# An expert loop whose transposes go from TensorE to VectorE, with the weight rows regrouped to match

## The reference

```python
xin = xf[buf_tok].reshape(nblk, MOE_BLOCK, D)          # xf = RMSNorm(x) * norm2_g
def expert_block(args):
    xb, e = args
    hh = xb @ w1[e] + b1[e]                            # 1024 -> 2048
    x_glu = jnp.minimum(hh[..., ::2], SWIGLU_LIMIT)
    x_lin = jnp.clip(hh[..., 1::2], -SWIGLU_LIMIT, SWIGLU_LIMIT)
    act = x_glu * jax.nn.sigmoid(SWIGLU_ALPHA * x_glu) * (x_lin + 1.0)
    return act @ w2[e] + b2[e]                         # 1024 -> 1024
```

## Time and profile before

| what | value |
|---|---|
| median of 3 runs | 1527.27 us (1527.02 to 1527.79) |
| profiled execution, first to last instruction | 1525.0 us |
| expert loop, first matmul to the last of block 32 | 431.65 to 1499.92 us |
| one block while nothing disturbs it | 33.14 us |
| TensorE busy | 1451.5 us, 95% of the span |
| moved by DMA | 452.72 MB, 297 GB/s over the span |
| DMA rate in the loop | 384 to 400 GB/s in most of 40 slices |

### The profile page before, as it was taken

The page is one execution under the profiler, slowest core; times in us unless marked ns, Lnnn a source line. Parts: engine busy times, 40 slices in busy tenths (PEclk is TensorE's granted clock), DMA queues, the critical chain, the costliest instruction groups (busy, mean ns, idle before and its releaser), DMA issues.

```text
span 1525.0 us, 33907 instructions
## 1 busy us (share of the span) xinstructions
PE 1451.5 (95%) x14155; PEld 644.4 (42%) x14155; DVE 412.5 (27%) x988; ACT 280.7 (18%) x545; POOL 244.5 (16%) x342
## 2 busy tenths in 40 slices
PE   6999989799589999999999999999999999999995
PEld 3344447444534433334443334444333444443332
DVE  1008152622432222223222223222222322222233
ACT  3413022431101111111111111111111111111112
POOL 0000000000002221112122111223111222221111
PEclk9999995799689999999999999999999999999997
DMA  9110000260559999999999999999999999999983
GB/s 359 45 49 0 0 25 25 83 261 0 221 190 364 384 388 394 399 394 398 391 388 388 397 399 400 396 386 392 390 396 394 400 398 378 393 387 392 388 324 118
DMA packets 103864, 452.72 MB, mean 297 GB/s; under 512 B 16543, under 2 KB 25175, under 8 KB 71076
## 3 DMA queue, kind: packets, MB, share of 16 engines
q1 hardware_dynamic: 82232, 426.54, 70.5%
q0 software_dynamic: 17728, 16.86, 5.5%
q10 hardware_dynamic: 3884, 9.04, 1.6%
HBM read 442.63 MB, written 18.91 MB: 303 GB/s over the span
## 4 chain that ended last, share of the span: by engine, by line
PE 84%; DMA 8%; DVE 5%; ACT 1%; issue 1%; POOL 0%; SPq 0%; DVEq 0%; POOLq 0%
PE bank L691 40%; PE bank L699 19%; DMA arena<-in_w 7%; PE bank L483 6%; PE bank L476 5%; PE bank L623 4%; PE bank L730 2%; PE bank L684 1%; PE bank L569 1%; PE bank L576 1%; PE bank L604 1%; DVE fixed L1085 1%; PE bank L632 1%; ACT fixed L902 1%; DVE arena L1120 1%
## 5 line engine op out<-in xcount | busy, mean ns | idle before, releaser
L691 PE MATMUL bank<-arena,fixed 128*32 128x512 f32 x6144 | 669.6, 594 | 3.8 <-DMA arena<-in_w 2.8
L691 PEld LDWEIGHTS bank<-arena,fixed 128*32 128x32 f32 x6144 | 202.9, 110 | 451.0 <-issue 445.7
L699 PE MATMUL bank<-arena,fixed 128*32 128x256 f32 x6144 | 351.4, 381 | 0.0
L1303 DVE TENSOR_TENSOR fixed<-bank,fixed 128x512 f32<-128x512 f32 x96 | 66.4, 692 | 788.0 <-PE bank L691 788.0
L699 PEld LDWEIGHTS bank<-arena,fixed 128*32 128x32 f32 x6144 | 189.7, 110 | 129.9 <-issue 10.7
L823 POOL DMA_INDIRECT sum_d<-fixed x96 | 150.5, 1568 | 15.1 <-issue 14.2
L976 ACT ACTIVATE fixed<-fixed 128x256 f32<-128x256 f32 x96 | 43.2, 450 | 560.6 <-DVE fixed L1304 560.6
L799 POOL COPY fixed<-fixed 96x1 int32 (+1 forms) x34 | 6.1, 179 | 635.2 <-PE bank L684 614.5
L786 POOL TENSOR_TENSOR fixed<-fixed 128x1 f32<-128x1 f32 x130 | 63.3, 487 | 205.5 <-ACT fixed L997 202.6
L483 PE MATMUL bank<-arena,fixed 128*128 128x512 f32 x192 | 85.7, 609 | 0.0
L476 PE MATMUL bank<-fixed,arena 128*128 128x512 f32 x192 | 82.8, 592 | 0.8 <-DVE fixed L1045 0.8
(11 more groups left out here) (191 smaller groups left out, 807.3 us busy)
## 6 DMA issues: line engine op xcount, KB each, us to landing
arena<-in_w SPq DMA_DIRECT2D x384, 1024.0 KB, 16.9
arena<-in_w_in SPq DMA_DIRECT2D x6, 2048.0 KB, 16.1
arena<-in_w_out SPq DMA_DIRECT2D x1, 4096.0 KB, 21.6
fixed<-rel_d ACTq DMA_DIRECT2D x8, 448.0 KB, 3.7
fixed<-in_x SPq DMA_DIRECT2D x4, 512.0 KB, 6.3
hn_d<-fixed ACTq DMA_DIRECT2D x1, 2048.0 KB, 7.0
sum_d<-fixed ACTq DMA_DIRECT2D x1, 2048.0 KB, 13.2
fixed<-sum_d SPq DMA_DIRECT2D x4, 512.0 KB, 5.1
```

Source lines behind the costliest of these rows:

```text
L691: m = pe.matmul(bank[r][GR * j:GR * (j + 1), :], XT[:, k, GR * r:GR * (r + 1)], W1[:, k, 512 * j:512 * (j + 1)], start=k == 0, stop=k == N ...
L699: m = pe.matmul(bank[3 + r // 2][GR * j:GR * (j + 1), 256 * (r % 2):256 * (r % 2 + 1)], ATT[:, r, c, f2, :], W2[:, 2 * f2 + c, 256 * j:256 ...
L1303: step(v.tensor_tensor(z, bank[r][:, :], B1T, ALU.add))
```

## The change

VectorE now does both kinds of transpose, in blocks of 32 x 32. Such a transpose turns each 32 x 32 block in its place: from `ACTV`, partition 32j + i of `ATT` gets value 256j + 8i + f for f = 0 to 7 when the source columns are read with stride 8, which is value 8p + f for partition p. So the rows of a weight matrix that belong to one partition must be the eight consecutive ones 8p to 8p + 7. The weight loads follow: partition p of slot k gets row 8p + k instead of 128k + p.

- Tokens: `XG` holds quarter rows. Three indirect DMAs of 128 quarter rows (1 KB) each gather a block's tokens, by the scatter's table `SID`; the table `TOK` and its instruction go. Three VectorE transposes (128 x 256) write `XT`.
- Activations: after each group's product, VectorE transposes `ACTV[:, r, :]` into `ATT[:, r]`. TensorE's transposes and ScalarE's copies go.
- TensorE's products run in plain order r = 0, 1, 2, each over f = 0 to 3.
- Weights: `w1` slot k is read as 128 rows of 8 KB that lie 64 KB apart (before: 1 MB in one stretch). A piece of `w2` is read as 128 runs of 8 KB (two consecutive rows), 32 KB apart (before: 256 rows of 4 KB, in one stretch of 1 MB).
- `norm2_g` is now multiplied into `HN` (one `scalar_tensor_tensor` in place of a `tensor_scalar`, L1196 before), from a broadcast row `G2` (512 KB, a new DMA on ScalarE's queue between the router's weights and its bias); the scaling of the router's weights goes.

```diff
-    XG = view(fixed, o_qk, D, parts=SLOTS)
-    XT = view(fixed, o_qk + 1024, NK, SLOTS)
+    XG = view(fixed, o_qk, NG, D // NJ)
+    XT = view(fixed, o_qk + 1024, NG, NK, GR)
...
             for k in range(NK):
-                             w1[bass.ds(e, 1), k * P:(k + 1) * P, :].rearrange("e p n -> (e p) n")
+                             w1[bass.ds(e, 1), :, :].rearrange("e (p k) n -> (e p) k n", k=NK)[:, k, :]
...
             for f in range(NF // 2):
-                             w2[bass.ds(e, 1), 2 * f * P:(2 * f + 2) * P, :].rearrange("e (a p) n -> p (e a) n", p=P)
+                             w2[bass.ds(e, 1), :, :].rearrange("e (p f) n -> (e p) f n", f=NF)[:, 2 * f:2 * f + 2, :]
...
-            act_transposes(0)
-            x_transposes(16 * g + 32)
-            pe.wait_ge(s_at, NG * g + 1)
...
+            for r in range(NG):
+                pe.wait_ge(s_at, NG * g + r + 1)
+                for f2 in range(NF // 2):
+                    if r == 0:
+                        pe.wait_ge(s_w2[f2], 16 * g + 16)
+                    m = product(r, f2)
+                    if r == 2:
+                        m.then_inc(s_used, 1)
+                if r == 1:
+                    m.then_inc(s_yf, 1)
...
-            pool.indirect_dma_start(out=XG, out_offset=None, in_=hn_d.ap(),
-                                    in_offset=bass.IndirectOffsetOnAxis(GI, 0),
+            for r in range(NG):
+                pool.indirect_dma_start(out=XG[:, r, :], out_offset=None, in_=quarters,
+                                        in_offset=bass.IndirectOffsetOnAxis(GI[:, r:r + 1], 0),
...
+        act.dma_start(G2, bass.AP(norm2_g.tensor, 0, [[0, P], [1, D]])).then_inc(s_g2, 16)
...
-                v.tensor_scalar(HN[:, t, :], X[:, t, :], st4[:, t:t + 1], None, ALU.mult).then_inc(s_xn, 1)
+                v.scalar_tensor_tensor(HN[:, t, :], X[:, t, :], st4[:, t:t + 1], G2,
+                                       ALU.mult, ALU.mult).then_inc(s_xn, 1)
...
+            for r in range(NG):
+                v.transpose(XT[:, r, :, :], XG[:, r, :].rearrange("p (i k) -> p k i", k=NK)).then_inc(s_xt, 1)
             v.stream_shuffle(B1T, B1Q, [0] * GR).then_inc(s_b1p, 1)
...
+                v.transpose(ATT[:, r, :, :], ACTV[:, r, :].rearrange("p (i f) -> p f i", f=NF)).then_inc(s_at, 1)
```

More of the change, by code:

```diff
@@ L250, in encoder_block @@
     ACTV = view(fixed, o_nt + 2304, NG, FF // NJ)
-    ATT = view(fixed, o_gqk, NG, 2, NJ, GR)
+    ATT = view(fixed, o_gqk, NG, NF, GR)
     YN = view(fixed, o_gqk + 768, NG, D // NJ)
@@ L264, in encoder_block @@
     VT = view(fixed, take(NV), NV)
-    GI = view(fixed, take(1), 1, parts=SLOTS, dt=I32)
+    GI = view(fixed, o_l + NCL + 2 * NG * COLS, NG, dt=I32)
     SI = view(fixed, take(NG), NG, dt=I32)
@@ L284, in encoder_block @@
     JUNK = view(fixed, o_a, D)
+    G2 = view(fixed, o_a, D)
     ident = CF[:, CI:CI + P]
@@ L675, in _ @@
         assert done[0] == len(jobs)
[L678 to L686, removed]
         def hidden(r, k):
             for j in range(NJ):
-                m = pe.matmul(bank[r][GR * j:GR * (j + 1), :], XT[:, k, GR * r:GR * (r + 1)],
+                m = pe.matmul(bank[r][GR * j:GR * (j + 1), :], XT[:, r, k, :],
                               W1[:, k, 512 * j:512 * (j + 1)], start=k == 0, stop=k == NK - 1)
@@ L724, in _ @@
                     m.then_inc(s_hf, 1)
[L726 to L731, removed]
-            act_transposes(0)
-            x_transposes(16 * g + 32)
-            pe.wait_ge(s_at, NG * g + 1)
[L737 to L752, removed]
+            for r in range(NG):
[8 more added lines that the diff above has]
+                    m.then_inc(s_yf, 1)
         nb = pe.value_load(EMAP[0:1, MAXB:MAXB + 1], min_val=E, max_val=MAXB)
         pe.wait_ge(s_yn, NG * nb)
-        pe.wait_ge(s_xt, 2 * nb + 2)
+        pe.wait_ge(s_xt, NG * nb + NG)
         pe.wait_ge(s_b2, 16)
@@ L789, in _ @@
         pool.memset(B1Q, 0.0).then_inc(s_b1z, 1)
-        last_token, last_row = (pool.to_reg(n - 1) for n in (SEQ, SEQ * NJ))
+        last_row = pool.to_reg(SEQ * NJ - 1)
         pool.wait_ge(s_hst, 16)
@@ L797, in gather @@
         def gather(column, copied):
[L799 removed]
+            pool.tensor_copy(GI, SID[:, :, column].rearrange("p a b -> p (a b)")).then_inc(s_idx, 1)
             pool.wait_ge(s_idx, copied)
             hold(NG)
[L802 to L804 removed]
+            for r in range(NG):
+                pool.indirect_dma_start(out=XG[:, r, :], out_offset=None, in_=quarters,
+                                        in_offset=bass.IndirectOffsetOnAxis(GI[:, r:r + 1], 0),
+                                        bounds_check=last_row, oob_is_err=False).then_inc(s_gath, 16)
+        quarters = hn_d.ap().rearrange("t (j n) -> (t j) n", j=NJ)
         gather(slice(0, 1), 2)
[L807 removed]
+        pool.wait_ge(s_xt, NG)
         gather(slice(1, 2), 3)
[L809 removed]
         pool.wait_ge(s_acc0, 16)
@@ L1168, in _ @@
         v.wait_ge(s_rw, 48)
-        for k in range(NK):
-            ins = v.tensor_scalar(RWs[:, k, :], RWs[:, k, :], VT[:, V2 + k:V2 + k + 1], None, ALU.mult)
-        ins.then_inc(s_rw2, 1)
+        v.wait_ge(s_g2, 16)
         io = CF[:, CIO:CIO + E]
@@ L1262, in _, with next_tokens @@
         wait_empty(v, ("rep",))
[L1264 to L1276, removed]
+        def next_tokens(n):
+            v.wait_ge(s_b1, 16 * n)
+            v.wait_ge(s_gath, 16 * NG * n)
+            for r in range(NG):
+                v.transpose(XT[:, r, :, :], XG[:, r, :].rearrange("p (i k) -> p k i", k=NK)).then_inc(s_xt, 1)
             v.stream_shuffle(B1T, B1Q, [0] * GR).then_inc(s_b1p, 1)
         v.wait_ge(s_b1z, 1)
-        next_tokens(0, 16)
+        next_tokens(1)
         blocks = v.value_load(EMAP[0:1, MAXB:MAXB + 1], min_val=E, max_val=MAXB)
```

40 lines of the change are left out of this document (13 added, 27 removed).

## The result

The changed kernel takes 1490.5 us (1488.9 to 1491.0, 4 runs) where the kernel before takes 1527.4: a ratio of 0.9755, 95% interval 0.9742 to 0.9769. The gain is 37 us; 11.6 had been forecast (1515.7), and the range ended at 1500. The direction and the bound were right, the size was a third of what came.

What follows compares the result with a forecast made beforehand. The prediction took the DMA stream of weights to bound the loop. Start +3.8, HN +0.5, stream -10.4, block 1 -1.9 and tail -3.6 sum to -11.6 us: span 1525.0 to 1513.4, median 1515.7, range 1500 to 1534.

Steps and rivals of the forecast that it cites:

- The bound: Loop: the DMA stream of weights takes 33.9 us a block and bounds it; TensorE as the bound had chance 0.04.
- nearly all off the path: TensorE's transposes in the loop: removing them saves TensorE 57 us over 32 blocks, nearly all without effect on the time.
- The signs I had named: Loop, if right: blocks of 33.0 to 33.6 us, TensorE idle about 2 us in each from the first quarter on.
- The stream itself: Weight loads over the loop's 31 blocks: -10.4 us in sum; no gain there had chance 0.16.
- block 1's gap: Block 1, where the DMA ran dry before W2's slots came free: first piece free earlier, -1.9 us.
- The run length of w2: W2 loads in runs of 8 KB instead of 4 KB: -0.24 us per block, -7.4 in all, bounds -10 and 0.
- The address pattern: Weight loads with 64 KB or 32 KB pitch: taken as 0, 31 us either way; a slower stream had chance 0.15.
- The third part, the gathers: Quarter rows spread each token over four partition groups, loading DMA engines more evenly: -3 us, bounds -7.5 and +5.
- The start: Before the first hidden matmul: later first gather, three gathers, VectorE transposes, +3.8 us (2.6 to 5.3); HN ahead, +0.5.
- VectorE's cover: VectorE's transposes in each block, 0.37 to 0.74 us each, are done before TensorE needs them: no cost.
- GpSimd: "Nothing": Three gathers queue in front of each block's scatters; the last scatter still waits for TensorE's end: no cost.
- The tail: Last block: TensorE ends 8.0 us behind the last W2 landing instead of 11.6, -3.6 us.

## Why the prediction was wrong, step by step

**The bound** was named rightly: the stream, not TensorE, although TensorE was busy 95%. TensorE's 2.2 us less per block gave no 70 us. But I called them "nearly all off the path". They are off it only as long as the stream stays slower than 33.14 us a block. The three runs on the kernel before show that taking them away is what lets a faster stream count: with them, each of three ways to speed the stream ended at 1522. The signs I had named came near: blocks of 32.53 us (said 33.0 to 33.6), TensorE idle 1.4 us in each (said about 2), from block 11 of 32 on (said the first quarter).

**"The stream itself", the step that failed.** Its sum of -10.4 over 31 blocks, with -1.9 for block 1's gap, was -38.6. It had three parts. The run length of w2 was sized at -7.4 and measured 10.1. The address pattern was taken at 0 and measured 0 (1489.1 against 1490.5). The Trainium skill's page ("DMA: Bandwidth & Descriptors", Latency and other measured facts) gives figures for row pitches from 512 KiB up and none below; what the prediction calls full rate there is 207 GB/s against 214. That nothing is lost at 64 KB was my extrapolation, and these runs bear it out. The third part, the gathers, I treated only as load: the same bytes, perhaps spread better over the engines, -3 with bounds of -7.5 and +5. The run with the old gather puts them at 28.4, and 20.6 of it go with the number of partitions alone. The effect that I had priced did not come: the engines end as unevenly as before, with a share of 0.12 up to 1452. I never asked what the gather does to the packets of the weights beside it. The row that shows it was there to be read: windows of 2 us behind each gather, at 336 and 305 GB/s with the share at 1.0. My windows were whole blocks, and an average of 390 hides a dip of 4 us. The two measured parts come to 38.5, near the 38.6; but they were taken one at a time out of the changed kernel, and no run has the kernel before without TensorE's transposes alone.

**The start:** +3.8 and +0.5 forecast, the first hidden matmul came +3.2 later. Rows of the changed kernel, GpSimd's first and last gather and VectorE's transposes:

```profile
427.82 1.12 POOL L775 DMA_INDIRECT fixed<-hn_d,fixed  x1 [0.17 <-issue]
...
430.58 1.00 POOL L775 DMA_INDIRECT fixed<-hn_d,fixed  x1 [0.30 <-issue]
...
433.02 1.67 DVE L1230 STREAM_TRANSPOSE fixed<-fixed 128x256 f32<-128x256 f32 x3 [5.66 <-DMA fixed<-hn_d,fixed]
```

The first gather was issued 2.3 us later (425.50 to 427.82), where +1.2 for `SID` and +0.5 for HN had been forecast. A gather of 128 quarter rows takes 1.0 to 1.1 us, not 1.4; one of 96 rows of 4 KB in the changed kernel takes 1.06 and one over 128 partitions 1.09, so the time doesn't go by the rows. The data came 3.2 later (429.83 to 433.02), and transposing took 1.8 as before, where 1.3 was forecast. The delayed router's bias was hidden, as said: VectorE waited for it until 341.91 instead of 340.17, and the first transposes of HN moved from 353.96 to 354.34 only.

**VectorE's cover** held, in price and place:

```profile
L1266 DVE STREAM_TRANSPOSE fixed<-fixed 128x256 f32<-128x256 f32 x96 | 62.7, 654 | 3.3
L1230 DVE STREAM_TRANSPOSE fixed<-fixed 128x256 f32<-128x256 f32 x99 | 55.6, 613 | 5.7 <-DMA fixed<-hn_d,fixed 5.7
```

0.65 us is between my 0.37 and 0.74, nearer the upper one, and TensorE never waits for them in the loop. The 0.62 estimated from the Trainium skill ("VectorE: DVE Perf Modes", The three transpose paths) is near it; the page's figure is for bf16, and these transposes are float32.

**GpSimd: "Nothing"** was wrong for the last block. I had the gathers end 9 us behind the hidden part's end, with the scatters free to follow; they ended 9.9 behind 1450.6, and then three scatters of 2 us each stood in a row behind TensorE's end. In the loop that is covered, at the end nothing covers it: 2.9 us. Turning the order round gave back 1.8 of them.

**The tail** of the stream was right in mechanism and near in size, 8.6 us behind the last landing for the 8.0 forecast.

**The range** failed for the same reason as the sum: its lower end took the bounds of the known effects and left no room for one that I hadn't looked for.

## What to carry to other kernels

Two bounds within 2% of each other hide each other: a faster stream alone gave 5 us, TensorE's transposes gone beside the old gather 9 (w2's longer runs included), both 37. Before judging a change to one of them, work out what each alone would allow. When the DMA's share is full, look at its rate too, in windows as short as the smallest transfer in the loop and over many iterations, not in one: here a stretch at full share with a lower rate was a transfer that held up its neighbours, and a single block showed it less surely than 27. And where a gather runs beside a stream of loads, try it over all 128 partitions, with its rows laid so that empty ones are spread evenly.

## What the runs showed of the hardware that was not expected

- In the kernel before, a gather of some 64 rows of 4 KB, declared over 96 partitions, pulled the weight stream beside it from 423 to 336 and 305 GB/s for 4 us with the share at 1.0; declared over 128 partitions it left it at 412 and 408. In the changed kernel the same step made 31 blocks 20.6 us shorter, though there a dip of 2 us stayed, at 299 GB/s with a share of 0.86.
- Loads in runs of 8 KB instead of 4 KB: 0.33 us less per 4.19 MB. A pitch of 64 KB between 8 KB rows: no difference.
- In the run with the old gather TensorE waited for weights 24 times, and behind eight of these waits, of 2.07 to 3.50 us, the granted clock fell. Windows around the restart at 1440.72, behind a wait of 2.68 us:

```profile
1438.00:1440.70 2.70, 0.04 (x3) 0.01 (x1) 0.00 (x0) 0.00 (x0) 0.00 (x0) 1.00 1.05 419
1440.70:1444.00 3.30, 3.28 (x20) 1.17 (x24) 0.00 (x0) 0.00 (x0) 0.00 (x0) 0.58 1.01 427
1444.00:1450.20 6.20, 6.20 (x60) 2.17 (x56) 4.51 (x12) 0.90 (x2) 0.00 (x0) 0.95 1.02 418
```

It was near the lower of its two levels (1.2 GHz; 0.58 of full speed in the window) for some 3 us, and 72 hidden matmuls took 9.63 us instead of 7.93. The length of the wait doesn't decide it: seven others, of 2.03 to 3.03 us, left the 72 matmuls at 7.93, and in the run over 128 partitions one of 1.98 was followed by 9.63. In the changed kernel the waits reach 1.95 us and none was. In the loop the 1.7 us cost little, since the stream is the bound; behind the last wait, at 1440.72, nothing takes them back.
